# Block 2's first mixing of a two-block transformer on one Trainium2 core: memory's queries computed first, convolution's factors by weights, memory's heads between weight pieces

## What is computed

```python
h = rmsnorm(x, mix_norm[layer])
mkv = (mem_h @ mem_w_kv[layer]).reshape(b, m, 2, MEM_HEADS, HEAD_DIM)
mem_k = rmsnorm(mkv[:, :, 0], mem_k_gain[layer]); mem_v = mkv[:, :, 1]
z = h @ a_w_in[layer]                         # 1024 x 2560
gate_b, gate_c, u = split(z[..., :3 * 768], 3); v = gate_c * u
y_tok = gate_b * causal_conv_of_3_taps(v, conv_w)      # per channel
q = rmsnorm(z[..., 3 * 768:], q_gain) * HEAD_DIM ** -0.5     # 4 heads of 64
y_mem = softmax(q @ mem_k.T) @ mem_v          # 256 memory rows
x = x + concatenate([y_tok, y_mem]) @ w_out[layer]
```

## Time and profile before

| | |
|---|---|
| runs, median (lowest to highest of 3) | 1505.63 us (1504.1 to 1509.23) |
| profiled execution | 1505.66 us, span of its instructions 1503.9 us |
| TensorE clock granted, mean | 0.972 of full |
| busy: PE, PE weight loads, DVE, ACT, POOL | 94%, 89%, 59%, 45%, 12% |
| DMA | 225.1 MB, mean 150 GB/s |

### The profile page before, as it was taken

The page is one execution under the profiler, slowest core; times in us unless marked ns, Lnnn a source line. Parts: engine busy times, 40 slices in busy tenths (PEclk is TensorE's granted clock), DMA queues, the critical chain, the costliest instruction groups (busy, mean ns, idle before and its releaser), DMA issues.

```text
span 1503.9 us, 24454 instructions
## 1 busy us (share of the span) xinstructions
PE 1419.8 (94%) x10298; PEld 1336.3 (89%) x10298; DVE 882.5 (59%) x1192; ACT 683.3 (45%) x987; POOL 180.9 (12%) x174
## 2 busy tenths in 40 slices
PE   7998999999889999999999885989999999999998
PEld 6997999999889889999997674989999888899997
DVE  5476655555655676555566755545546776665554
ACT  5533544334447245444345542334445565454442
POOL 2001210000110022100021200111111311020000
PEclk9999999999999899999999995999999999999999
DMA  7722255565363124775544360244554441155562
GB/s 218 207 87 83 85 197 189 176 192 180 111 182 108 57 85 141 251 228 175 194 140 164 98 214 28 90 163 169 177 199 158 156 160 57 47 190 184 170 196 83
DMA packets 159657, 225.10 MB, mean 150 GB/s; under 512 B 19081, under 2 KB 127625, under 8 KB 159548
## 3 DMA queue, kind: packets, MB, share of 16 engines
q1 hardware_dynamic: 159548, 223.55, 45.9%
HBM read 222.44 MB, written 1.09 MB: 149 GB/s over the span
## 4 chain that ended last, share of the span: by engine, by line
PE 82%; DVE 10%; issue 4%; ACT 3%; POOL 1%; DMA 0%; DVEq 0%; ACTq 0%; SPq 0%; POOLq 0%
PE ps L2366 17%; PE ps L2367 16%; PE ps L2368 16%; PE ps L2358 4%; PE ps L2359 4%; PE ps L2360 4%; PE ps L2645 2%; PE ps L2646 2%; PE ps L2647 2%; DVE xT L1456 2%; DVE w_lo L1419 2%; ACT w_hi L802 1%; PE ps L2997 1%; DVE h L1471 1%; PE ps L2879 1%
## 5 line engine op out<-in xcount | busy, mean ns | idle before, releaser
L1419 DVE TENSOR_TENSOR w_lo<-raw,w_hi 128x2048 fp32r<-128x2048 f32 (+4 forms) x206 | 472.2, 2298 | 277.4 <-ACT w_hi L802 275.1
L2366 PE MATMUL ps<-xT,w_hi 128*128 128x256 f32 x1600 | 463.1, 289 | 8.0 <-DVE w_lo L1419 6.9
L802 ACT ACTIVATE w_hi<-raw 128x2048 fp32r<-128x2048 f32 (+4 forms) x206 | 386.5, 1879 | 162.6 <-PE ps L2368 80.1
L2367 PE MATMUL ps<-xT,w_hi 128*128 128x256 f32 x1600 | 456.1, 285 | 0.0
L2368 PE MATMUL ps<-xT,w_lo 128*128 128x256 f32 x1600 | 455.8, 285 | 0.0
L2366 PEld LDWEIGHTS ps<-xT,w_hi 128*128 128x128 f32 x1600 | 310.5, 194 | 12.6 <-DVE w_lo L1419 7.5
L2367 PEld LDWEIGHTS ps<-xT,w_hi 128*128 128x128 f32 x1600 | 310.5, 194 | 0.6
L2368 PEld LDWEIGHTS ps<-xT,w_lo 128*128 128x128 f32 x1600 | 310.3, 194 | 0.0
L2366 PE MATMUL ps<-hT,w_hi 128*128 128x256 f32 x640 | 182.7, 285 | 5.4 <-DVE hT L1919 4.6
L2367 PE MATMUL ps<-hT,w_hi 128*128 128x256 f32 x640 | 182.1, 284 | 0.0
L2368 PE MATMUL ps<-hT,w_lo 128*128 128x256 f32 x640 | 182.0, 284 | 0.0
(11 more groups left out here) (332 smaller groups left out, 2041.7 us busy)
## 6 DMA issues: line engine op xcount, KB each, us to landing
raw<-in_w_up_dram SPq DMA_DIRECT2D x54, 1024.0 KB, 5.4
raw<-in_w_down_dram SPq DMA_DIRECT2D x54, 1024.0 KB, 5.1
raw<-in_w_gate_dram SPq DMA_DIRECT2D x22, 1024.0 KB, 5.3
raw<-in_w_in_dram SPq DMA_DIRECT2D x14, 1024.0 KB, 5.3
raw<-in_a_w_in_dram SPq DMA_DIRECT2D x10, 1024.0 KB, 5.4
raw<-in_w_o_dram SPq DMA_DIRECT2D x8, 1024.0 KB, 4.9
raw<-in_w_ple_gate_dram SPq DMA_DIRECT2D x8, 1024.0 KB, 5.0
raw<-in_w_out_dram SPq DMA_DIRECT2D x8, 1024.0 KB, 4.8
```

What stands on the lines that cost most here:

```text
L802: nc.scalar.activation(w_hi[:, p % RH, 0:piece_width(p)], raw[:, p % RR, 0:piece_width(p)], ACT.Copy).then_inc(E["hi_ready"], 1)
L1419: nc.vector.tensor_tensor(w_lo[:, p % RH, 0:w], raw[:, p % RR, 0:w], w_hi[:, p % RH, 0:w].bitcast(F32), ALU.subtract).then_inc(E["lo_ready ...
L2366: nc.tensor.matmul(out_, w[0][:, kk, c], x(0, k), start=start and j == 0, stop=False, skip_group_check=True)
L2367: nc.tensor.matmul(out_, w[0][:, kk, c], x(1, k), start=False, stop=False, skip_group_check=True)
```

## The change

The plan gets two stages in place of `a_in`: one piece with memory's 256 query columns, and nine with 256 convolution columns each, in the order gate_c, u, gate_b for every two blocks of channels. `first_mixing` on each engine replaces what `a_in`, the units and `attention` did. The queries are made by tokens, the nine others by weights without a factor: two of the three get the token factor from a row spread over the partitions (`along`, squared for gate_c * u in `along2`), on the way out of PSUM. Six transposed units go. Memory's heads, their scores, transposes and values, stand between half pieces. The output weights for memory's channels are the first piece of `w_out`, and their blocks of `xT` the first two. POOL's `norm` order is unchanged. `CONV_BANKS` says which bank holds which factor.

```diff
         if l == 0:
-            add(("a_in", l), wide("a_w_in_2", 0, A_IN))
+            add(("mq", l), [sub("a_w_in_2", 0, 0, KD, (3 * CONV, MEM_W))])
+            add(("conv", l), [sub("a_w_in_2", 0, 0, KD, (c + 2 * P * j, 2 * P)) for j in range(3) for c in (CONV, 2 * CONV, 0)])
         else:
             add(("kv", l), wide("w_kv_shared_2", 0, 6 * NSA_G * HD))
             add(("memq", l), [sub("b_w_in_2", 0, 0, KD, (B_IN - MEM_W, MEM_W))])
...
-        add(("w_out", l), [sub("w_out_2", l, 2 * i, 2, (0, D)) for i in (range(KD // 2) if l == 0 else W_O)])
+        add(("w_out", l), [sub("w_out_2", l, 2 * i, 2, (0, D)) for i in W_O])
...
-SPREAD = [("attn", 0), ("ffn", 0), ("ple", 0), ("attn", 1), ("ffn", 1), ("ple", 1), ("final", 0), ("mlp", 0)]
+SPREAD = [("attn", 0), ("ffn", 0), ("ple", 0), ("attn", 1), ("ffn", 1), ("ple", 1), ("final", 0), ("mix", 0),
+          ("mlp", 0)]
...
-        z0 = take(NT, A_IN)
+        z0 = take(NT, MEM_W)
+        along1, along2 = take(S), take(S)
+        cx = take(2, S)
...
-                    for u in plain(kmem[:, l, :, :], 0, 2, memkT[:, l, :, :], COLS[("mem_k_gain_2", l)])]
-
-        def conv_units():
-            return plain(z0, 0, 6, bconv) + plain(z0, 2 * CONV, 6, vconv[:, :, 2:S + 2])
+                    for u in plain(kmem[:, l, :, :], 0, 2, memkT[:, l, :, :], COLS[("mem_k_gain_2", l)], 2 * l)]
         def mem_query_units():
-            return plain(z0, 3 * CONV, 2, mq0, COLS[("mem_q_gain_2", 0)])
+            return plain(z0, 0, 2, mq0, COLS[("mem_q_gain_2", 0)], 0)
...
+        CONV_BANKS = ((6, 7, 1), (4, 5, 6), (0, 2, 1))
...
-                pool.wait_ge(E["tt_a"], 6)
-                pool.wait_ge(E["tt_d"], 5)
+                pool.wait_ge(E["tt_a"], 3)
+                pool.wait_ge(E["tt_d"], 2)
...
+            def first_mixing():
+                jobs, o0 = mem_jobs(0), n["O"]
+                used(("mq", 0), 0)
+                wide_evac(("mq", 0), MEM_W, z0, ("mix", 0), ahead_=False)
+                used(("conv", 0), 0)
+                evac_units(mem_units())
+                ahead(ACT.Exp)
+                used(("conv", 0), 1)
+                act.wait_ge(E["r_mm"], SPREAD.index(("mix", 0)) + 1)
+                nc.scalar.activation(along2, PS[3][:, S:2 * S], ACT.Square)
+                nc.scalar.activation(along1, PS[3][:, S:2 * S], ACT.Copy).then_inc(E["R_ready"], 1)
+                used(("conv", 0), 2)
+                evac_units(mem_query_units())
+                def exps(i):
+                    J, G = n["J"] + i, n["G"]
+                    act.wait_ge(E["l_done"], NT * (J + 1))
+                    act.wait_ge(E["pt_done"], J - 1)
+                    for t in (1, 0):
+                        c = t * S
+                        nc.scalar.activation(Pb[:, J % 2, c:c + S], PS[i % 2][:, c:c + S], ACT.Exp, bias=nmax[:, J % 2, t:t + 1],
+                                             accum_out=rows[:, 4 * (G % 2) + i, t:t + 1]).then_inc(E["e_done"], 1)
+                exps(0)
+                exps(1)
+                used(("conv", 0), 3)
+                exps(2)
+                used(("conv", 0), 4)
+                exps(3)
+                used(("conv", 0), 5)
+                used(("conv", 0), 6)
+                n["tr"] += 1
+                act.wait_ge(E["tr_done"], n["tr"])
+                for k in range(2):
+                    nc.scalar.activation(xT[:, 0, place(("out", 0), k), :], PS[3][:, S * k:S * k + S], ACT.Copy
+                                         ).then_inc(E["xhi"], 1)
+                used(("conv", 0), 7)
+                for b in range(6):
+                    if b == 0:
+                        act.wait_ge(E["piece_used"], FIRST[("conv", 0)] + 9)
+                    act.wait_ge(E["conv_y"], b + 1)
+                    nc.scalar.activation(xT[:, 0, place(("out", 0), 2 + b), :], yconv[:, b, :], ACT.Copy).then_inc(E["xhi"], 1)
+                    if b == 1:
+                        used(("conv", 0), 8)
...
-                    wide_evac(("a_in", 0), A_IN, z0, ("mix", 0))
-                    ahead(ACT.Exp)
-                    evac_units(mem_units() + conv_units() + mem_query_units())
-                    for b in range(6):
-                        act.wait_ge(E["conv_y"], b + 1)
-                        nc.scalar.activation(xT[:, 0, place(("out", 0), b), :], yconv[:, b, :], ACT.Copy).then_inc(E["xhi"], 1)
-                    attention(mem_jobs(0))
-                    rounded_T(2, lambda part_, k: xT[:, part_, place(("out", 0), k), :], None, at=6)
+                    first_mixing()
...
+            def first_mixing():
+                p = FIRST[("conv", 0)]
+                jobs, o0 = mem_jobs(0), n["O"]
+                used(("mq", 0), 0)
+                wide_evac(("mq", 0), MEM_W, z0, ("mix", 0), True, ahead_=False)
+                on_diagonal(("mix", 0))
+                dve.wait_ge(E["wide_a"], n["wide"])
+                dve.wait_ge(E["wide_d"], n["wide"])
+                link(nc.vector.tensor_tensor(LbF[:, 0:512].rearrange("p (t d) -> p t d", t=NT), z0, z0, ALU.mult))
+                nc.vector.tensor_reduce(hss[:, 0:8], LbF[:, 0:512].rearrange("p (a d) -> p a d", d=HD), AX_X,
+                                        ALU.add).then_inc(E["hn_sq"], 1)
+                used(("conv", 0), 0)
+                evac_units(mem_units())
+                dve.wait_ge(E["hn_r"], 2)
+                for t in range(NT):
+                    qv = z0[:, t, :].rearrange("p (a d) -> p a d", d=HD)
+                    i = nc.vector.scalar_tensor_tensor(qv, qv, HD ** -0.5, hrs[:, 4 * t:4 * t + 4].unsqueeze(2)
+                                                       .broadcast_to([P, MEM_H, HD]), op0=ALU.mult, op1=ALU.mult)
+                i.then_inc(E["qn_ready"], 1)
+                used(("conv", 0), 1)
+                def two(bank):
+                    return PS[bank][:, :].rearrange("p (b s) -> p b s", b=2)
+                def product(j):
+                    if j == 0:
+                        nc.vector.memset(vconv[:, :, 0:2], 0.0)
+                        dve.wait_ge(E["R_ready"], SPREAD.index(("mix", 0)) + 1)
+                    dve.wait_ge(E["piece_used"], p + 3 * j + 2)
+                    link(nc.vector.tensor_tensor(cx, two(CONV_BANKS[j][0]), along2.unsqueeze(1).broadcast_to([P, 2, S]), ALU.mult))
+                    link(nc.vector.tensor_tensor(vconv[:, 2 * j:2 * j + 2, 2:S + 2], two(CONV_BANKS[j][1]), cx, ALU.mult))
+                def third(j):
+                    dve.wait_ge(E["piece_used"], p + 3 * j + 3)
+                    nc.vector.tensor_tensor(bconv[:, 2 * j:2 * j + 2, :], two(CONV_BANKS[j][2]),
+                                            along1.unsqueeze(1).broadcast_to([P, 2, S]), ALU.mult).then_inc(E["cv_ev"], 1)
+                def taps(j):
+                    for k in range(3):
+                        for b in (2 * j, 2 * j + 1):
+                            w = COLS[("a_conv_w_2", k)] + b
+                            src, y = vconv[:, b, k:k + S], yconv[:, b, :]
+                            if k == 0:
+                                i = nc.vector.tensor_scalar(y, src, col[:, w:w + 1], None, ALU.mult)
+                            else:
+                                i = nc.vector.scalar_tensor_tensor(y, src, col[:, w:w + 1], y, op0=ALU.mult, op1=ALU.add)
+                        link(i)
+                    dve.wait_ge(E["cv_ev"], j + 1)
+                    for b in (2 * j, 2 * j + 1):
+                        nc.vector.tensor_tensor(yconv[:, b, :], yconv[:, b, :], bconv[:, b, :], ALU.mult
+                                                ).then_inc(E["conv_y"], 1)
+                def rests_(j):
+                    for b in (2 * j, 2 * j + 1):
+                        n["x"] += 1
+                        dve.wait_ge(E["xhi"], n["x"])
+                        at = place(("out", 0), 2 + b)
+                        nc.vector.tensor_tensor(xT[:, 1, at, :], yconv[:, b, :], xT[:, 0, at, :].bitcast(F32),
+                                                ALU.subtract).then_inc(E["xlo"], 1)
+                def logits(i):
+                    J = n["J"] + i
+                    dve.wait_ge(E["s_done"], J + 1)
+                    dve.wait_ge(E["e_done"], NT * (J - 1))
+                    for t in (1, 0):
+                        nc.vector.tensor_reduce(nmax[:, J % 2, t:t + 1], PS[i % 2][:, t * S:t * S + S], AX_X, ALU.max, negate=True
+                                                ).then_inc(E["l_done"], 1)
+                def move_pT(i):
+                    J = n["J"] + i
+                    dve.wait_ge(E["pt_done"], J + 1)
+                    dve.wait_ge(E["o_done"], o_before(o0, i))
+                    nc.vector.tensor_copy(PTb[:, J % 2, :], PS[2][:, :]).then_inc(E["pte_done"], 1)
+                evac_units(mem_query_units())
+                product(0)
+                used(("conv", 0), 2)
+                third(0)
+                logits(0)
+                logits(1)
+                move_pT(0)
```

(112 more changed lines are left out.)

66 lines of the change are left out of this document (32 added, 34 removed).

## The result

The changed kernel takes **1493.65 us** in the median of six runs (1477.96 to 1500.52) against 1506.72 us (six runs, 1504.1 to 1510.76) for the kernel before in the same rounds: ratio 0.987, 95% interval 0.9844 to 0.9896. That ratio is not the one of these two medians (0.991): it leaves out the two slowest executions of the changed kernel as disturbed, 1500.31 and 1500.52 us, and goes by 1487.2 us, the median of the other four. The forecast was 1474.3 us. The sign is right, but 13 us (19 by the four) came where 31 were forecast, and the median of the six lies 11 us above the range. The profiled execution took 1500.52 us around a span of 1498.7 us, so it is at the slow end; an execution of 1496.55 us, profiled later (*again*), shows the same fall of the clock. The six differ in the clock: 1477.96 us came with a mean granted clock of 0.982, 1500.31 us with 0.964.

The account below looks back on a forecast made before the run. TensorE bounds the kernel (82% of the span), with a serial tail of small work after block 2's input product. Output product earlier -30.1, faster start -1.2: -31.3 us from 1505.63 gives 1474.3 us, range 1470.5 to 1483.

Parts of the forecast that it names:

- Order of weights and shape of the product: New mixing: queries' piece first, 7.8 us, then nine convolution pieces by weights, 5.76 us each, 51.8 us together.
- Small work and supply: TensorE's head work between pieces costs 12.3 us; VectorE's weight splits arrive in time except about 1.0 us of stall.
- the term of -30.1: Block 2's output product starts at 909.7 instead of 939.8, saving 30.1 us.
- The stall ahead of the first scores: TensorE waits about 1.0 us near 870 for VectorE's third factor before memory's first scores.
- The 2.28 us wait: TensorE's old wait for a split weight piece at 856.19, forecast to go with its slow matmuls.
- The end: VectorE's remaining convolution work hides behind the output product by at least 2 us; uncovered it would cost about 10 us.
- the -1.2 term: Output product's first 12 matmuls start at the fast clock, 0.12 instead of 0.21 us each, saving 1.2 us.
- rival 1: VectorE's in-order queue is late in the mixing, so heads wait: 8 us late, 1482 us; chance 0.12.
- rival 2: The tail only moves: some 10 us of convolution rests precede the output product's second piece, 1484 us; chance 0.05.
- Nothing behind the output product changes; it ended the path before and does so after: Stages behind the output product were costed at no difference, so its -31.3 us reach the end.
- Rival 3: Small waits in the new mixing hold TensorE at 1.2 GHz: 49 us lost, 1524 us, slower; chance 0.03.
- sign of being right: TensorE's clock stays above 0.95 from 837 on, one listed mark that the forecast holds.

Follow-up runs that it names:

- again: The changed kernel unaltered, timed again as a base for the others: 1498.53 us, ratio 0.994.
- fill8: The changed kernel plus eight unread 256-column matmuls beside each of layer 2's heads 8 and 9: 1480.25 us, ratio 0.9826.
- fill8_14: fill8 plus an unread 128-column matmul ahead of each of the 12 thin products of layer 2's head 14: 1481.72 us, ratio 0.9836.
- fill8_mid: fill8 with head 14's two output-product units put between its 12 thin products instead of behind them: 1477.32 us, ratio 0.9807.
- early1_shift14: early1 plus 14 idle matmuls (1.7 us) ahead of the first layer's output product: 1472.55 us, ratio 0.9783.
- shift14: The changed kernel plus 14 idle matmuls (1.7 us) between the new mixing and the output product: 1486.2 us, ratio 0.9873.
- early1: The changed kernel with VectorE scaling one four-head group's outputs before, not behind, 0.5 us of gelu work at layer 2's head 8: 1469.94 us, ratio 0.9767.
- early1_lag: early1 plus two extra reciprocals on VectorE ahead of that group's own reciprocal: 1495.58 us, ratio 0.9918.
- pad4: The changed kernel plus four unused reciprocals in VectorE's idle time at layer 2's head 7: 1469.7 us, ratio 0.9769.

## Why the prediction was right, and where it was wrong

- **Order of weights and shape of the product: right.** The 432 matmuls by weights take 0.12 us each (the first piece's 48 start from 845.21 to 850.85). The queries' piece followed VectorE as described and took the 7.8 us forecast (1.1 of them waits). It began at 837.43 where 836.8 was taken as unchanged, so the convolution began at 845.2 against 844.6.
- **Small work and supply: right.** Output product at 909.34 against 909.7 forecast, so -30.5 for the term of -30.1. Some luck is in it: the start was 0.6 us later than assumed, and the small work and the stall took 1.0 us less than their 13.3. The stall ahead of the first scores was 0.65 us for 1.0 (in the forecast's walk the split of piece 5 ends at 866.1, where its own terms, 863.3 + 2.29, give 865.6); the product with a broadcast row 0.68 us for 0.7. The 2.28 us wait went.
- **The end: right.** No wait for xT or its weights inside the output product, and its first matmuls are 0.12 us apart (the -1.2 term).
- **Rivals 1 and 2 did not occur.** The waits on w_lo and Pb between pieces that rival 1 needed, and those for xT in the output product that rival 2 needed, are not there.
- **"Nothing behind the output product changes; it ended the path before and does so after": the step that failed.** The forecast put the stages behind the output product at no difference, and the clock differed in two of them. In its favour, 33.45 us stood at layer 2, 2.15 more than forecast. 1.5 of these arose between 31.80 and 33.30, at the start of the up-projection, where the kernel before ran at the lower clock for 3.4 us (973.4 to 976.8) and the changed one did not. Against it, the heads of layer 2 lost 28.3 us in the profiled execution: a wait of TensorE for VectorE that was 0.20 us before was 0.53 us there, and about 65 us at the lower clock followed. This step, and not a term of the sum for the mixing, put the median 19.4 us above the forecast.
- **Rival 3 had the right mechanism in the wrong place.** It put the lower clock into the new mixing, where the clock stayed at 1.00 through waits of 0.65 us, and took layer 2's clock of 1.00 as evidence that heads are safe. That row showed only that they were so with a wait of 0.20 us. The forecast's sign of being right, a clock above 0.95 from 837 on, held to 950 and failed in layer 2 (and for 6.8 us behind the output product, at 950 to 957, where the kernel before has as long a stretch). The forecast had no term for the place where that wait could grow: the range of 1470.5 to 1483 holds the medians of four of the variants (*fill8*, *fill8_14*, *fill8_mid*, *early1_shift14*), two more lie just below it, and the changed kernel itself lies above. The Trainium skill's warning quoted there (frequent micro-idles between groups of matmuls make the clock swing) fits layer 2 only in part: one wait of 0.53 us was followed by one long stretch at the lower level, not by swings; the new mixing's waits were followed by neither.
- **With the cause removed** the same change gives 1469.9 us, 35.9 below the kernel before in its rounds, where the forecast said 31.3.

Left open: why VectorE paused 0.24 us, what sets the length of a fall from one execution to the next, and whether the wait does harm at another distance from the clock's last rise. The pause stands ahead of the same instruction in each profiled run whose VectorE instructions are those of the changed kernel (*again*, *fill8*, *fill8_14*, *fill8_mid*, *shift14*), whatever its time, and in none with another order or count (*early1*, *early1_lag*, *pad4*). So it goes with the instruction's place in VectorE's stream; what in that place causes it was not tried.

## What to carry to other kernels

An edit of one stage can change a wait of a few tenths of a microsecond in a stage 300 us behind it that it does not touch. Look there for thin stretches of TensorE (bare heads, transposes, few columns) that have even a 0.2 us wait in them, and take the wait away in the same edit, by another order (*early1*) or by work put into it (*fill8*, which kept a later fall), since here 0.3 us more of wait cost 28 us at the lower clock. When the executions of a kernel spread by 20 us and their times go with the granted clock, search the trace for the first matmul that is twice as long, and look at the wait ahead of it.

## What the runs showed that was not expected

- A wait of 0.38 to 0.67 us was followed by 31 to 65 us at the lower clock in layer 2, in one to three pieces, though TensorE was busy for nearly all of it (58.99 of 60 us in the changed kernel). In the changed kernel the clock rose again at 1274.3, behind four 256-column fp32 matmuls (2.07 us) and the first three matmuls of head 20's four units of the output product; heads 10 to 19, with one or two units each, had not brought it back.
- The clock also fell with no wait at all: over 24 matmuls of 32 columns, 3.75 us, TensorE counted busy throughout (*fill8*).
- The five falls at heads 8 and 9 stand 252.6 us behind the clock's last rise, and the four in kernels with fillers 269.7 us, though the rises lie up to 33 us apart (956.4 to 989.7, 954.6 to 989.1). The executions without the longer wait have the same rise and no fall.
- Work that nobody reads made the kernel faster: 16 matmuls on the bounding engine saved 18 us (*fill8*), four instructions on VectorE 29 us (*pad4*, both against the median of *again*). 14 matmuls elsewhere gave 12 us (*shift14*), but there the executions overlap with those of the changed kernel.
- A pause of 0.24 us on VectorE that belongs to a place in its stream of instructions and goes when four are added ahead of it.
